# A hybrid attention and RWKV-7 block: narrow first projections in buffers of their own, second projections between big products, and no reads for the meta tokens

## What is computed

```python
xx = jnp.pad(h, ((0, 0), (1, 0), (0, 0)))[:, :-1] - h
xs = h[None] + xx[None] * mu[:, None, None, :]
rkv = jnp.einsum('nbtd,nde->nbte', xs[:3], w_rkv)
r, k, v = rkv[0], rkv[1], rkv[2]
xv, xw, xa, xg = xs[2], xs[3], xs[4], xs[5]
w_log = -jax.nn.softplus(-(w0 + jnp.einsum('btl,ld->btd', jnp.tanh(xw @ w1), w2)).astype(jnp.float32)) - 0.5
v = v + (v_first - v) * jax.nn.sigmoid(v0 + (xv @ v1) @ v2)
a = jax.nn.sigmoid(a0 + (xa @ a1) @ a2)
g = jax.nn.sigmoid(xg @ g1) @ g2
...
def step(S, inp):
    r_t, w_t, k_t, v_t, a_t, b_t = inp
    sa = jnp.einsum('bhij,bhj->bhi', S, a_t)
    S = (S * w_t[:, :, None, :] + sa[..., None] * b_t[:, :, None, :]
         + v_t[..., None] * k_t[:, :, None, :])
    return S, jnp.einsum('bhij,bhj->bhi', S, r_t)
...
return rms_norm(h[:, N_META:], final_norm)
```

## Time and profile before

| | us |
|---|---|
| time, median of 3 runs | 1644.88 (1640.95 to 1644.9) |
| profiled execution, span | 1638.5 |
| profiled execution, time of its own | not listed apart from the three runs |
| PE busy | 1567.2 (96%) |
| VectorE busy | 852.3 (52%) |
| ScalarE busy | 637.0 (39%) |
| POOL busy | 156.7 (10%) |
| front of the time mix | 710.5 to 942.3 |
| chunks | 942.3 to 1177 |

### The profile page before, as it was taken

The page is one execution under the profiler, slowest core; times in us unless marked ns, Lnnn a source line. Parts: engine busy times, 40 slices in busy tenths (PEclk is TensorE's granted clock), DMA queues, the critical chain, the costliest instruction groups (busy, mean ns, idle before and its releaser), DMA issues. The chain is left out here.

```text
span 1638.5 us, 35327 instructions
## 1 busy us (share of the span) xinstructions
PE 1567.2 (96%) x15881; PEld 1410.4 (86%) x15881; DVE 852.3 (52%) x1201; ACT 637.0 (39%) x880; POOL 156.7 (10%) x180
## 2 busy tenths in 40 slices
PE   6999998999999999999999989999789999999997
PEld 5998987999999999989988978888558888888886
DVE  5675665544433444677566545545485444344432
ACT  3654654332212223455566333333244322122322
POOL 3100100001000015000000411101010010001100
PEclk9999999999999999998999989999999999999999
DMA  4112121333332333662222100000303333233331
GB/s 132 53 59 72 53 72 46 91 91 90 105 89 78 91 90 115 176 183 71 62 72 59 39 19 4 4 4 5 106 28 98 94 91 114 81 90 102 100 94 64
DMA packets 225814, 126.41 MB, mean 77 GB/s; under 512 B 8856, under 2 KB 220976, under 8 KB 225408
## 3 DMA queue, kind: packets, MB, share of 16 engines
q1 hardware_dynamic: 225360, 124.07, 25.6%
q10 hardware_dynamic: 304, 0.08, 0.0%
HBM read 117.71 MB, written 6.42 MB: 76 GB/s over the span
## 5 line engine op out<-in xcount | busy, mean ns | idle before, releaser
L125 ACT ACTIVATE w_hi<-w_raw 128x1024 fp32r<-128x1024 f32 (+1 forms) x200 | 224.3, 1122 | 548.0 <-PE psg L785 305.8
L785 PE MATMUL psg<-x_hi,w_hi 128*128 128x264 f32 (+1 forms) x1080 | 350.2, 324 | 1.8 <-DVE w_lo L129 1.8
L785 PE MATMUL psg<-x_lo,w_hi 128*128 128x264 f32 (+1 forms) x1080 | 350.4, 324 | 0.0
L785 PE MATMUL psg<-x_hi,w_lo 128*128 128x264 f32 (+1 forms) x1080 | 349.6, 324 | 0.0
L129 DVE TENSOR_TENSOR w_lo<-w_raw,w_hi 128x1024 fp32r<-128x1024 f32 (+1 forms) x200 | 261.9, 1310 | 139.8 <-ACT w_hi L125 139.6
L785 PEld LDWEIGHTS psg<-x_hi,w_hi 128*128 128x128 f32 x1080 | 202.8, 188 | 20.1 <-DVE w_lo L129 2.2
L785 PEld LDWEIGHTS psg<-x_lo,w_hi 128*128 128x128 f32 x1080 | 202.8, 188 | 17.4 <-issue 0.2
L785 PEld LDWEIGHTS psg<-x_hi,w_lo 128*128 128x128 f32 x1080 | 203.3, 188 | 16.7
L1248 PE MATMUL psg<-mid_hi,w_hi 128*128 128x264 f32 (+1 forms) x528 | 170.8, 323 | 2.5 <-DVE w_lo L129 2.5
L1248 PE MATMUL psg<-mid_lo,w_hi 128*128 128x264 f32 (+1 forms) x528 | 170.0, 322 | 0.0
L1248 PE MATMUL psg<-mid_hi,w_lo 128*128 128x264 f32 (+1 forms) x528 | 169.4, 321 | 0.0
(11 more groups left out here) (389 smaller groups left out, 3182.7 us busy)
## 6 DMA issues: line engine op xcount, KB each, us to landing
w_raw<-in_w_ffn_in_dram SPq DMA_DIRECT2D x88, 512.0 KB, 3.8
w_raw<-in_w_ffn_out_dram SPq DMA_DIRECT2D x40, 704.0 KB, 4.6
w_raw<-in_w_qkv_dram SPq DMA_DIRECT2D x24, 512.0 KB, 3.8
w_raw<-in_w_rkv_dram SPq DMA_DIRECT2D x24, 512.0 KB, 4.1
w_raw<-in_w_o_attn_dram SPq DMA_DIRECT2D x8, 512.0 KB, 4.1
w_raw<-in_w_o_rwkv_dram SPq DMA_DIRECT2D x8, 512.0 KB, 4.2
v_first<-v_pair SPq DMA_DIRECT2D x8, 264.0 KB, 2.0
res_kept<-res SPq DMA_DIRECT2D x1, 2112.0 KB, 7.8
```

Of the source, the lines that this page charges most:

```text
L125: k.nc.scalar.activation(k.w_hi[j][:, 0:kt, :], k.raw[j][:, 0:kt, :], ACT.Copy).then_inc(k.hi_ready[j].h, 1)
L785: done = k.nc.tensor.matmul(k.psg[:, 2 * j + c, 0:size], w[:, t, :], x, start=t == first and n == 0, stop=t == last and n == 2)
```

## The change

- v1 and w1 are no units any more. They are loaded ahead of the first MLP stage into buffers of their own (`small_sync`), split there by `small_high` and `small_low`, and multiplied by `small_row` into banks 2 and 3 of `psx`, as 128-row products with 32 or 64 output columns. 30 units are left, and all later ones move by one or two.
- The first halves of V_UNITS[0] and V_UNITS[1] are multiplied before the late rows; the late rows serve v1 and V_UNITS[0] in turn, then V_UNITS[1] finishes.
- `second` is cut into rows. `unit_beside` runs three of them, then a big unit with one row of six between its tiles (three products of 264, or of 512) until the eight are done: v2 beside the third v unit, w2 beside the third k unit, a2 beside the second r unit.
- ScalarE copies v out of PSUM (`v_copy`), and `v_evict` works in SBUF. The table for the sigmoids is loaded ahead of the first hidden row.
- r is computed for 512 tokens, as one product of 512 columns instead of two of 264 (`spans`, `r_evict`).
- SP loads v_first ahead of the spill of the residual, both behind two more weight loads.
- Chunk 0 has no r side: no `y_state_product`, no `chain_y`, no `w_product` (the state is zero; wt is -av), no `reads`, and `quads` of half the columns.
- A few semaphores are merged; this changes no order.

```diff
-V1, V2, W1, W2, G1, A1, A2 = 0, 3, 10, 13, 16, 22, 24
-V_UNITS = (1, 2, 4, 5, 6, 7, 8, 9)
-K_UNITS = (11, 12, 14, 15, 18, 19, 20, 21)
-R_UNITS = (23, 25, 26, 27, 28, 29, 30, 31)
-FRONT_UNITS = 32
+V2, W2, G1, A1, A2 = 2, 11, 14, 20, 22
+V_UNITS = (0, 1, 3, 4, 5, 6, 7, 8)
+K_UNITS = (9, 10, 12, 13, 16, 17, 18, 19)
+R_UNITS = (21, 23, 24, 25, 26, 27, 28, 29)
+FRONT_UNITS = 30
...
+    def small_high(self, act):
+
+        act.wait_ge(self.small_in.h, 2 * 16)
+        for n in range(2):
+            self.k.nc.scalar.activation(self.r.small_hi[n][:], self.r.small_raw[n][:], ACT.Copy).then_inc(self.small_r.h, 1)
+
+    def small_low(self, dve):
+
+        dve.wait_ge(self.small_r.h, 2)
+        for n in range(2):
+            self.k.nc.vector.tensor_tensor(self.r.small_lo[n][:], self.r.small_raw[n][:], self.r.small_hi[n][:].bitcast(F32),
+                                           ALU.subtract).then_inc(self.small_r.h, 1)
...
+    def spans(self, n):
+
+        return [(META, SEQ)] if n >= MIX_R else [(0, HALF), (HALF, HALF)]
...
-        sp.wait_ge(self.rs_r.h, 2)
-        sp.dma_start(k.res_kept, k.res[:]).then_inc(self.spilled.h, 16)
         for i in range(2, FRONT_UNITS):
             unit_load(k, sp, self.u0 + i, self.srcs[i], KT)
             if i == 3:
+                sp.wait_ge(self.rs_r.h, 2)
                 sp.dma_start(r.kk_in[:, :, PAD:TP], k.v_first).then_inc(self.vf_in.h, 16)
+                sp.dma_start(k.res_kept, k.res[:]).then_inc(self.spilled.h, 16)
...
+        def r_evict(m):
+            i = R_UNITS[m]
             self.wait_done(act, i)
-            nc.scalar.activation(r.hid_hi[0:rank, :].rearrange("p (a b) -> p a b", a=2), halves(k, (self.u0 + i) % 2)[0:rank],
-                                 ACT.Copy).then_inc(self.hid_h.h, 1)
+            nc.scalar.activation(r.rr[:, m, C:TP], k.psg[:, 2 * ((self.u0 + i) % 2), :], ACT.Copy)\
+                .then_inc(self.freed(i), 1)
...
-        hidden(V1, LORA['v'][2], 0)
+        nc.scalar.preload_act_table_set("sigmoid_and_others")
+        hidden_v()
+        v_copy(0)
         self.weights_hi(act, 2)
+        parts(8, 9)
+        v_copy(1)
         self.weights_hi(act, 3)
-        parts(8, 11)
+        parts(10, 11)
+        second(0, r.rr, vcol(k, 'v0'))
         self.weights_hi(act, 4)
-        second(0, r.rr, vcol(k, 'v0'))
-        self.weights_hi(act, 5)
         highs(8, 11)
         parts(12, 13)
-        self.weights_hi(act, 6)
+        v_copy(2)
...
-            i = V_UNITS[m]
-            j, out = (self.u0 + i) % 2, real(r.vv, m)
-            self.wait_done(dve, i)
+            first, out = r.kk_in[:, m, PAD:TP], r.vv[:, m, PAD:TP]
+            self.wait_freed(dve, V_UNITS[m] if m else V2)
+            nc.vector.tensor_tensor(first, first, out, ALU.subtract).then_inc(self.v_step.h, 1)
             dve.wait_ge(self.turn_r.h, m + 1)
-            nc.vector.tensor_tensor(out, real(r.kk_in, m), halves(k, j), ALU.subtract).then_inc(self.v_step.h, 1)
-            dve.wait_ge(self.v_step.h, 2 * m + 1)
-            nc.vector.tensor_tensor(out, out, real(r.rr, m), ALU.mult).then_inc(self.v_step.h, 1)
-            dve.wait_ge(self.v_step.h, 2 * m + 2)
-            nc.vector.tensor_tensor(out, out, halves(k, j), ALU.add).then_inc(self.freed(i), 1)
-
-        def hidden_low(i, rank, index):
+            dve.wait_ge(self.v_step.h, 3 * m + 1)
+            nc.vector.tensor_tensor(first, first, r.rr[:, m, PAD:TP], ALU.mult).then_inc(self.v_step.h, 1)
+            dve.wait_ge(self.v_step.h, 3 * m + 2)
+            nc.vector.tensor_tensor(out, out, first, ALU.add).then_inc(self.v_step.h, 1)
...
             for a, (w, x) in enumerate(((k.w_hi[j], hi), (k.w_hi[j], lo), (k.w_lo[j], hi))):
                 done = nc.tensor.matmul(k.psg[:, 2 * j + c, 0:size], w[:, t, :], x[:, at:at + size],
                                         start=t == 0 and a == 0, stop=t == KT - 1 and a == 2)
-            if t == KT - 1 and c == 1:
+            if t == KT - 1 and c == len(self.spans(n)) - 1:
...
+        def unit_beside(i, first, s, rank, which, lead):
+
+            second_begin(s)
+            for m in range(lead):
+                second_row(s, rank, which, m)
+            begin(i)
+            m = lead
+            for c in range(len(self.spans(first))):
+                for t in range(KT):
+                    row_products(i, first + t, c)
+                    if m < KT:
+                        second_row(s, rank, which, m)
+                        m += 1
...
-        begin(V1)
+        pe.wait_ge(self.small_r.h, 4)
         for t in range(KT):
             self.wait_low_half(pe, t, 0)
-            row_products(V1, t, 0)
+            small_row(0, LORA['v'][2], t, 0)
             if t == KT // 2:
                 second_sums()
-        begin(V_UNITS[0])
-        for t in range(KT):
-            row_products(V_UNITS[0], t, 0)
+        for i in V_UNITS[0:2]:
+            begin(i)
+            for t in range(KT):
+                row_products(i, t, 0)
         for t in range(KT):
             self.wait_low_half(pe, t, 1)
-            row_products(V1, t, 1)
+            small_row(0, LORA['v'][2], t, 1)
             row_products(V_UNITS[0], t, 1)
-        unit(V_UNITS[1], MIX_V)
-        self.wait_freed(pe, V1)
-        second(V2, LORA['v'][2], 0)
-        for i in V_UNITS[2:]:
+        for t in range(KT):
+            row_products(V_UNITS[1], t, 1)
+        pe.wait_ge(self.hid_l.h, 1)
+        unit_beside(V_UNITS[2], MIX_V, V2, LORA['v'][2], 0, 3)
+        for i in V_UNITS[3:]:
             unit(i, MIX_V)
-        unit_by_rows(W1, MIX_W)
+        pe.wait_ge(self.turn_r.h, KT)
+        for t in range(KT):
+            self.wait_low(pe, MIX_W + t)
+            for c in range(2):
+                small_row(1, LORA['w'][2], MIX_W + t, c)
         unit_by_rows(K_UNITS[0], MIX_K)
         unit(K_UNITS[1], MIX_K)
-        pe.wait_ge(self.hid_l.h, 1)
-        second(W2, LORA['w'][2], 1)
-        unit(K_UNITS[2], MIX_K)
+        pe.wait_ge(self.hid_l.h, 2)
+        unit_beside(K_UNITS[2], MIX_K, W2, LORA['w'][2], 1, 3)
...
-        second(A2, LORA['a'][2], 2)
-        unit(R_UNITS[1], MIX_R)
+        unit_beside(R_UNITS[1], MIX_R, A2, LORA['a'][2], 2, 3)
...
                 def reads(n, p, half):
+                    if n == 0:
+                        return
...
-                        dve.wait_ge(w_d.h, c + 1)
-                        nc.vector.scalar_tensor_tensor(wt[:], wy_ps, -1.0, av[q][:], ALU.mult, ALU.subtract)\
-                            .then_inc(wt_r.h, 1)
+                        if c:
+                            dve.wait_ge(w_d.h, c)
+                            nc.vector.scalar_tensor_tensor(wt[:], wy_ps, -1.0, av[q][:], ALU.mult, ALU.subtract)\
+                                .then_inc(wt_r.h, 1)
+                        else:
+                            nc.vector.tensor_scalar(wt[:], av[q][:], -1.0, None, ALU.mult).then_inc(wt_r.h, 1)
...
+                    size = P if n else C
                     for h, m, rows in heads[first:first + len(parts) * KT // 2]:
-                        last = mm(pair_ps[:, h % 2, (m % 4) * P:(m % 4) * P + P],
+                        last = mm(pair_ps[:, h % 2, (m % 4) * P:(m % 4) * P + size],
                                   bk[rows, m, :, :].rearrange("p a c -> p (a c)"),
-                                  ar[p][rows, m, :, :].rearrange("p a c -> p (a c)"), start=True, stop=True)
+                                  ar[p][rows, m, :, :].rearrange("p a c -> p (a c)")[:, 0:size], start=True, stop=True)
...
-                    w = (lambda m, rows: w_product(c, q, m, rows)) if chain else None
-                    y_state = (lambda m, rows: y_state_product(c, q, m, rows)) if chain else None
+                    w = (lambda m, rows: w_product(c, q, m, rows)) if c > 0 else None
+                    y_state = (lambda m, rows: y_state_product(c, q, m, rows)) if c > 0 else None
...
-                    if chain:
+                    if c > 0:
                         chain_y(c, q)
```

More of the change, by code:

```diff
@@ L1638, in scalar @@
         parts(28, 29)
[L1639 removed]
+        self.weights_hi(act, 14)
         k_evict(2)
@@ L1830, in vector @@
-        self.weights_lo(dve, 24)
+        self.weights_lo(dve, 20)
+        mixed(*range(40, 48))
+        self.weights_lo(dve, 21)
+        lowered(40, 42, 44, 46)
+        hidden_low(3, LORA['a'][2], halves(k, (self.u0 + A1) % 2)[0:LORA['a'][2]], self.freed(A1))
+        self.weights_lo(dve, 22)
         dve.wait_ge(self.sums_d.h, KT)
@@ L1934, in unit @@
             begin(i)
-            for c in range(2):
+            for c in range(len(self.spans(first))):
                 for t in range(KT):
```

298 lines of the change are left out of this document (171 added, 127 removed).

## The result

The changed kernel takes 1655.2 us (median of 20 runs, 1643.6 to 1683.5) against 1644.85 for the kernel before (20 runs, 1639.6 to 1653.2): a ratio of 1.0049, 95% interval 1.0027 to 1.0072. The ratio leaves out runs more than 1.5% above the fastest of their kernel, here three of the 20; the medians are those of all runs. It is slower by about half a percent, where I had forecast 1634.4 and a range up to 1646. The profiled execution took 1655.1 us with a span of 1653.3, and its mean granted clock is 0.970 where before it was 0.983.

The account below looks back on a forecast made before the run. PE, busy for 96% of the span, was taken as the bound, so only PE time or waits could pay. Gains of 1.9 + 3.3 + 1.5 + 2.0 + 1.8 = 10.5 us took 1644.9 to 1634.4, range 1627 to 1646.

Parts of the forecast that it names:

- (b): v's `second` and the unit beside it: 1.5 us stall, clock between full and half; gain 1.9 us including (a).
- (d): w1, two k units, w's `second`, third k unit: gain 3.3 us at full clock, 3.4 less if it falls.
- (e): a's `second` beside an r unit of 512 columns: gain 1.5 us, or a loss of 1.9 if the clock falls.
- The price of alternating: Changing product shape there and back on PE: taken as 0.30 us a pair, bounds nothing extra and 0.37.
- (a): To the end of the third product of v, late rows included: gain 3.5 us.
- (f): The other seven r units, at 512 columns: 5.56 us each against 5.84, gain 2.0 us.
- (g): The chunks, with less work in chunk 0 and half-width quads: gain 1.8 us, bounds 0.8 and 3.6.
- (c): The other v units: ScalarE's copies freeing PSUM are covered; 0.7 us taken off in the all-full-clock case alone.
- The rival that gave 1655 us: Narrow outputs bring the clock down too, in v's late rows and w1: 11.4 us more, 1655; chance 0.08.
- The rival with all three falls as before (1643.6): Clock falls at v's, w's and a's `second` as before: gain only 1.3 us; chance 0.20.

Follow-up runs that it names:

- e17: The changed kernel unchanged, timed anew on one chip beside the one with 64 increments: 1648.0 us, ratio 1.0033 to the kernel before.
- e14: The changed kernel with each second product's eight rows in one run and 64 semaphore increments where TensorE waits: 1629.5 us, ratio 0.9936 to before.
- e5: The kernel before with receptance for 512 tokens only, the meta tokens' set to zero, its chunk stage kept: 1648.2 us, ratio 1.0016.
- e1: The kernel before, unchanged, timed anew with the granted clock of each run: 1643.7 us.
- e6: The kernel before with the shorter chunk 0 of the change, receptance still for 528 tokens: 1641.5 us, ratio 0.9989.
- e8: As e7, but receptance for 512 tokens, the meta tokens' set to zero: 1641.9 us, ratio 0.9968 to the kernel before.
- e13: The kernel before with 192 semaphore increments at TensorE's start, which move the place of its issue waits: 1660.7 us.
- e7: The changed front with all eight second-product rows ahead of the unit, receptance for 528 tokens, chunk stage of before: 1638.0 us, ratio 0.9963.
- e16: As e14, but a2's rows again between the receptance unit's rows, three ahead and five between: 1630.3 us, ratio 0.9944 to before.
- e4: The changed kernel with all eight rows of each second product ahead of the unit, without increments: 1647.8 us, ratio 1.0018 to before.

## Why the prediction was wrong, by its steps

**The sum** said -10.5 us. At equal clock the change gives -3.4 and -4.0 (the first runs and e17; nothing and -2.8 with a slope of 0.34), and time at half clock takes back 10 to 14. Step by step, PE's windows of the same work in the two kernels, first (b), (d) and (e) of before, then of the changed one:

```profile
735.50:753.85 18.35, 16.79 (x97) 16.33 (x97) 10.43 (x14) 12.17 (x17) 0.00 (x0) 0.72 0.19 57
783.09:818.57 35.48, 33.55 (x243) 32.34 (x241) 20.19 (x27) 23.38 (x36) 0.00 (x0) 0.90 0.23 64
879.58:897.17 17.59, 16.63 (x101) 15.17 (x101) 9.01 (x6) 11.47 (x15) 0.00 (x0) 0.81 0.22 61
```
```profile
728.13:751.23 23.10, 21.46 (x97) 18.64 (x97) 9.50 (x13) 12.42 (x19) 0.00 (x0) 0.63 0.21 63
780.46:821.57 41.11, 39.37 (x243) 36.38 (x241) 20.87 (x29) 22.94 (x36) 0.00 (x0) 0.79 0.16 45
882.32:899.11 16.79, 15.17 (x78) 10.56 (x77) 5.57 (x5) 9.39 (x13) 0.00 (x0) 1.00 0.11 32
```

The forecast's front gains 8.7 us and its chunks 1.8. In the profiles the front loses 1.3, of which (d) alone makes 8.9 of the 10.0 between, and the chunk steps lose 15.6 (48.15 and 148.91 us against 49.31 and 163.33).

**The price of alternating and (a)** were too high for narrow columns. PE's timeline in v's late rows of the changed kernel:

```profile
718.96 0.28 PE L1984 MATMUL psg<-x_hi,w_lo 128*128 128x264 f32 x1
719.09 0.28 PE L2042 MATMUL psx<-x_hi,v_hi 128*32 128x264 f32 x1
719.21 0.28 PE L2042 MATMUL psx<-x_lo,v_hi 128*32 128x264 f32 x1
719.33 0.28 PE L2042 MATMUL psx<-x_hi,v_lo 128*32 128x264 f32 x1
719.45 0.29 PE L1984 MATMUL psg<-x_hi,w_hi 128*128 128x264 f32 x1
```

Going to 32 columns and back costs nothing, 0.12 us from each product to the next, against the 0.30 a pair that I took. (a) ended at 728.1, gain 6.4 us against 3.5; the 0.30 in each of eight rows and the 0.6 "for shapes" are 3.0 us that weren't there. For 64 rows the 0.37 of the earlier trace rows held, as PE's timeline shows at a2:

```profile
886.91 0.50 PE L1984 MATMUL psg<-x_hi,w_hi 128*128 128x512 f32 x1
...
887.81 0.39 PE L2018 MATMUL psx<-hid_hi,w_hi 64*128 64x264 f32 x1
888.04 0.28 PE L2018 MATMUL psx<-hid_lo,w_hi 64*128 64x264 f32 x1
...
888.74 0.50 PE L1984 MATMUL psg<-x_hi,w_hi 128*128 128x512 f32 x1
```

From 886.91 to 888.74 is 1.83 us; three products of 0.232 and six of 0.122 are 1.43, so a pair of changes costs 0.40. The rule of the drain in the Trainium skill, TensorEngine Tiling (Array Packing), Key Properties, agrees with the rows at 32 and 64 rows, not with those at 32 columns.

**(b) and (d) are the steps of the front that failed: the clock beside `second`.** (b) took for v a time between the full and the half clock. It lost 4.75 us (23.10 against 18.35) where the forecast's times have it lose 1.6, and only because (a) came out 2.9 better than forecast do the two together gain 1.7 us, near the 1.9 foretold: that is luck. In (b) the stall (1.64 us against 1.5) and the step at half clock were right (2.57 against 2.6, five from 732.81 to 745.68), but every step ran at half clock:

```profile
731.46 0.39 PE L2018 MATMUL psx<-hid_hi,w_hi 32*128 32x264 f32 x1 [1.64 <-ACT rr L1581]
...
732.81 0.59 PE L1984 MATMUL psg<-x_hi,w_hi 128*128 128x264 f32 x1
```

The products between the rows stretched the time in which products of 32 rows come by from 11 to 17.6 us, and the clock stayed at half for 17.1 us, where e14, with the rows in one run, has 13.7. So big products that would have run at 2.4 GHz behind it ran at 1.2 beside it. Five pairs of changes more come on top, at 0.59 us each at half clock (2.57 less nine products of 0.22). A loss of 3.5 us against one run, and nothing hidden for it: PE idles 1.64 us in both (window less busy), since the stall lies ahead of the unit.

**(d)** was forecast at full clock, a gain of 3.3 us, and lost 5.6 (41.11 against 35.48). It is the largest miss of the front. The clock was at half for about 17 us there against 7 before: the five steps took 12.3 us (802.67 to 814.94) and not 7.35, the 33 products behind them 6.6 (to 821.57) and not 4.0, and PE waited 1.1 us in a k unit for VectorE's x_lo (at 790.43), which the forecast had at nothing. Even the forecast's own price of a fall there, 3.4 us, was that of a fall as long as before. w1 itself was as said, 5.8 us. Against rows in one run (e14) the piece lost 4.7. **(e)** held: clock 1.00, and a gain, 0.8 us (16.79 against 17.59) and not 1.5.

**(f)** held: 5.77 us a unit instead of 6.06; e5's front is 230.3 us, e1's 232.9 with falls of the same length: eight units at 0.3. **(g)** held within its bounds, 0.8 to 3.6: -2.8 in the rest of e6. **(c)** held: 29.23 us for the other v units against 29.24.

**What no step had** is the chunk stage's clock. (g) counts the products and waits of the chunks and has no term for it; I looked for falls only where shapes change. The rival that gave 1655 us has the measured number by luck, by a wrong way: narrow outputs don't bring the clock down, w1 runs at 1.00. The rival with all three falls as before (1643.6) had the mechanism of (b) and (d), though not the length of the falls nor a's, and its rows, low clock while 32- and 64-row products run, deserved more than 0.20.

**What stays open**: why receptance at 512 columns, which ends before the chunks, brings some 20 us more at half clock (e5, e8). In e8's profile most of it lies in the chunks (clock 0.82 from 940 to 1180 us); e5's profile is of a run with 65 us at half clock and doesn't show where it lies. Open too is whether the cuts add to it only together with it. Shown is that it isn't the cuts alone, nor the place of the issue waits alone (e13), and that these longer falls cost what the change gains. Why the clock falls there stays open.

## What to carry to other kernels

Products with few rows belong in one short run: each pair of changes between them and 128-row products costs 0.4 us at full clock and 0.6 at half, and where they hold TensorE at half clock, full products put between them run at half clock too. Putting them between hides nothing when the wait lies ahead of the unit. Cutting work in one stage can move the clock of the next: read the granted clock of untouched stages before believing a gain, and split each run into time at half clock and the rest, since the rest shows 4 us where the medians show nothing (with the slope checked on each kernel's own runs). Here the narrow first layers are worth keeping (e7, 0.4% faster than before), the rows between are not for v and w, and for a they make no difference that the medians show (1629.5 and 1630.3). The two kernels so made with the 64 increments (e14, e16) are 0.6% faster than the kernel before; e4, which is e14 without the increments on another chip, is not told apart from it, and what the increments do there isn't shown.
